# ScalarE instead of GpSimd makes the high weights of twelve units of the delta net's projection

## The reference, cut to what matters

```python
u = rms_norm(h, norm_mix_pre[l])
proj = u @ w_in[l]
dq, dk, dv, dz, db, da, aq, ak, av = jnp.split(proj, split_points, axis=-1)
o_dn = gated_deltanet_group(dq, dk, dv, dz, db, da, conv_w[l], a_log[l], dt_bias[l], dn_out_norm[l])
o_at = axial_gqa_group(aq, ak, av, q_norm[l], k_norm[l])
```

## Time and profile before

| | |
|---|---|
| median of 3 runs | 1503.74 us (1500.91 to 1503.95) |
| the profiled execution | 1504.27 us |
| its span | 1502.2 us |
| TensorE busy | 1393.9 us (93%) |
| VectorE busy | 744.8 us (50%) |
| ScalarE busy | 430.5 us (29%) |
| GpSimd busy | 767.2 us (51%) |
| mean granted clock of TensorE | 0.968 |
| `w_hi` by GpSimd | 188 units, 1071 ns each |
| `w_hi` by ScalarE | 16 units |
| `w_lo` by GpSimd | 204 units, 2530 ns each |

### The profile page before, as it was taken

How to read it: one execution, slowest core, us unless ns; L and a number is a source line. 1 busy time by engine, 2 the same in 40 slices (tenths; PEclk the granted TensorE clock), 3 DMA queues, 4 the chain that set the end, 5 groups by cost and what they waited for, 6 DMA issues and landing times.

```text
span 1502.2 us, 20334 instructions
## 1 busy us (share of the span) xinstructions
PE 1393.9 (93%) x7550; PEld 1144.9 (76%) x7550; DVE 744.8 (50%) x1113; ACT 430.5 (29%) x842; POOL 767.2 (51%) x443
## 2 busy tenths in 40 slices
PE   6999799898999999999899999868989999999996
PEld 4877577677888887888798888648867888888884
DVE  7968566644554457111767886497525111211112
ACT  3253344323121212111344444443423111111111
POOL 5444443345666666666343532405264666666661
PEclk9999899999999999999999999987999999999998
DMA  4321221112322222232111111000031322222221
GB/s 175 101 95 60 67 71 57 57 62 76 117 98 97 93 93 96 96 98 98 46 68 43 57 45 56 29 1 2 9 104 52 102 98 98 98 99 96 92 77 56
DMA packets 31739, 113.86 MB, mean 76 GB/s; under 512 B 3520, under 2 KB 3904, under 8 KB 31424
## 3 DMA queue, kind: packets, MB, share of 16 engines
q1 hardware_dynamic: 31536, 112.85, 22.6%
q10 hardware_dynamic: 144, 0.18, 0.0%
HBM read 110.92 MB, written 2.10 MB: 75 GB/s over the span
## 4 chain that ended last, share of the span: by engine, by line
PE 85%; DVE 10%; ACT 3%; issue 2%; DMA 0%; DVEq 0%; ACTq 0%
PE ps L1025 42%; PE ps L1225 18%; PE ps L1365 6%; PE ps L1044 3%; ACT arena L549 3%; PE ps L1058 2%; PE ps L1245 1%; PE ps L1339 1%; PE ps L1065 1%; PE ps L1168 1%; DVE arena L1665 1%; DVE arena L2038 1%; PE ps L1319 1%; PE ps L1157 1%; DVE arena L2136 1%
## 5 line engine op out<-in xcount | busy, mean ns | idle before, releaser
L470 POOL TENSOR_TENSOR w_lo<-raw,w_hi 128x1024 fp32r<-128x1024 f32 x204 | 516.0, 2530 | 66.1 <-ACT w_hi L549 50.4
L465 POOL TENSOR_SCALAR w_hi<-raw 128x1024 fp32r<-128x1024 f32 x188 | 201.4, 1071 | 565.3 <-PE ps L1025 190.1
L1025 PE MATMUL ps<-h_hi,w_hi 128*128 128x512 f32 (+1 forms) x976 | 376.7, 391 | 4.2 <-DVE arena L2284 2.2
L1025 PE MATMUL ps<-h_lo,w_hi 128*128 128x512 f32 (+1 forms) x976 | 369.8, 384 | 0.0
L1025 PE MATMUL ps<-h_hi,w_lo 128*128 128x512 f32 (+1 forms) x976 | 369.6, 384 | 0.0
L1025 PEld LDWEIGHTS ps<-h_hi,w_hi 128*128 128x128 f32 x976 | 182.4, 189 | 50.0 <-issue 12.1
L1025 PEld LDWEIGHTS ps<-h_lo,w_hi 128*128 128x128 f32 x976 | 182.1, 189 | 37.9 <-issue 2.7
L1025 PEld LDWEIGHTS ps<-h_hi,w_lo 128*128 128x128 f32 x976 | 182.1, 189 | 36.1
L549 ACT ACTIVATE arena<-ps 128x512 f32<-128x512 f32 (+7 forms) x205 | 96.5, 505 | 279.1 <-PE ps L1025 41.9
L549 ACT ACTIVATE arena<-arena 128x512 f32<-128x512 f32 (+6 forms) x191 | 101.4, 534 | 217.7 <-DVE arena L2284 134.3
L1225 PE MATMUL ps<-g_hi,w_hi 128*128 128x512 f32 x400 | 155.7, 389 | 0.9 <-DVE arena L1897 0.9
(11 more groups left out here) (279 smaller groups left out, 1888.5 us busy)
## 6 DMA issues: line engine op xcount, KB each, us to landing
raw<-in_w_stream SPq DMA_DIRECT2D x204, 512.0 KB, 3.5
xT<-in_x_t SPq DMA_DIRECT2D x2, 1056.0 KB, 7.3
out<-xT SPq DMA_DIRECT2D x8, 256.0 KB, 2.1
C<-in_cst SPq DMA_DIRECT2D x1, 576.0 KB, 10.0
arena<-in_cst SPq DMA_DIRECT2D x1, 528.0 KB, 4.9
arena<-in_pos SPq DMA_DIRECT2D x1, 256.0 KB, 3.9
V<-in_vec ACTq DMA_DIRECT2D x1, 174.5 KB, 6.0
band<-in_cst SPq DMA_DIRECT2D x1, 160.5 KB, 3.7
```

Of the source, the lines that this page charges most:

```text
L465: pool.tensor_scalar(w_hi[j][:], raw[j % 2][:], 1.0, 1.0, ALU.mult, ALU.mult).then_inc(S["pool_step"], 1)
L470: pool.tensor_tensor(w_lo[j][:], raw[j % 2][:], w_hi[j][:], ALU.subtract).then_inc(split_done[j], 1)
L1025: last = mm(dst[p], w[:, k, :], h[:, k, cols], start=(k == 0 and n == 0), stop=(k == KT - 1 and n == 2))
```

## The change

`LATE_HIGH` is (30, 33): in rounds 30, 31 and 32, units 120 to 131, GpSimd no longer makes the high part; it waits for `w_high` and makes the low part alone. ScalarE makes the high part of unit `U_DN2 + d + 4` at the end of `dn_copy(d)`, for d = 0 to 11 (for d from 12 on `dn_copy` returns before). Rounds 30 to 33 of GpSimd are written out instead of running in a loop, and later waits for `pool_step` count the three rounds that are left out.

```diff
+        LATE_HIGH = (U_DN2 // 4 + 1, U_DN2 // 4 + 4)
...
-            def split(i):
+            def split(i, late=False):
...
                     if isinstance(i, int) and 1 <= i < HIGH_ROUNDS:
                         pool.wait_ge(S["w_high"], 4 * i + j - 3)
+                    elif isinstance(i, int) and LATE_HIGH[0] <= i < LATE_HIGH[1]:
+                        pool.wait_ge(S["w_high"], 4 * (HIGH_ROUNDS - 1) + 4 * (i - LATE_HIGH[0]) + j + 1)
                     else:
...
-                            pool.wait_ge(S["pool_step"], 4 * i + (j + 1 - 4 * (HIGH_ROUNDS - 1)))
+                            skipped = HIGH_ROUNDS - 1 + (LATE_HIGH[1] - LATE_HIGH[0] if late else 0)
+                            pool.wait_ge(S["pool_step"], 4 * i + (j + 1 - 4 * skipped))
...
-            rep(pool, n0, split, HIGH_ROUNDS)
+            rep(pool, n0 - 1, split, HIGH_ROUNDS)
+            split(n0 - 1)
...
-            with pool.Fori(n0, n, 1) as i:
+            for i in range(n0, n - 1):
                 split(i)
+            split(n - 1, late=True)
...
             with pool.Fori(n, N_UNITS // 4, 1) as i:
-                split(i)
+                split(i, late=True)
...
                 a(y5, x5[:, d % 2, 2:L + 2], ACT.Copy, scale=vcol("dconv", 24 + d)).then_inc(S["c_act"], 1)
+                weight_high(U_DN2 + d + 4)
```

## The result

The changed kernel takes 1505.74 us in the median of 12 runs (1503.58 to 1510.00), the kernel before 1502.99 (12 runs). The ratio is 1.0023, with a 95% interval from 1.0012 to 1.0034: 2 to 5 us slower. I had forecast 0.4 us faster.

What follows compares the result with a forecast made beforehand. TensorE, busy 93% of the span, was taken as the bound. +1.34 (start) - 1.8 (steps 3 and 4) + 0.1 (step 11) + 0 (plain steps) = -0.4 us gave 1503.4 us against the median 1503.74; range 1499.8 to 1506.6.

Steps and rivals of the forecast that it cites:

- The plain step: Ordinary step of the projection loop with the second attention: stays at 10.03 us, costing 0, at most 0.1 us.
- Rival B: ScalarE's copy of the turned probabilities comes late and delays TensorE's turn each step: about +6 us, 1510; chance 0.11.
- C: Rival: VectorE is freed of the high part in every step, up to 1491 us, 1499 given; chance 0.09.
- Rival A: GpSimd wins the tie with VectorE; steps 3 and 4 gain only 0.2 us: +1.5, 1505.3; chance 0.22.
- the tie of step 3: VectorE's convolution step against GpSimd's low part near 825 us; if GpSimd wins, only 0.2 us is gained.
- Step 11: Loop step where VectorE also squares a tile and slack is gone: lateness of 0.07 to 0.4, +0.1 us taken.
- The start, pause: Loop start, TensorE waiting for VectorE's scaling: low part moves back, TensorE restarts 1.34 us later (bounds 0.96 to 1.35).
- The start, clock: TensorE's lower clock after the start's pause: expected the same as before; up to 0.5 us might come back.
- Steps 3 and 4: Convolution steps meeting GpSimd's gate products: 1.2 us shorter pause plus part of 1.25 us of clock; -1.8 taken (0.2 to 2.2).
- The sum: Whole kernel: +1.34 start, -1.8 steps 3 and 4, +0.1 step 11, 0 plain steps: -0.4 us, 1503.4; chance 0.58.
- if the clock falls in other places than before: One of the listed signs that the forecast is wrong, about TensorE's clock; no size given.
- The range: Whole kernel: 1499.8 to 1506.6 us, from bounds -1.7 and +2.5, run spread (2.8 below the median) and part of B.

Runs made afterwards that it cites:

- e5: Kernel before plus one ScalarE copy of 128x1024 into unused space ahead of the first exponentials, GpSimd's work unchanged; 1503.2 us, ratio 0.9998.
- e13: Kernel before plus one ScalarE copy of 128x512 in step 9, delaying TensorE about 0.5 us; 1504.8 us, ratio 1.0016.
- e15: Kernel before plus two ScalarE copies of 128x1024, in steps 8 and 9, delaying TensorE about 2.0 us; 1506.5 us, ratio 1.0024.
- e4: The change, but ScalarE makes unit 120's high part behind the first two heads' exponentials; 1502.7 us, ratio 0.9991 to the kernel before.
- e6: Kernel before plus three ScalarE copies (one 128x1024, two 128x528) ahead of the first exponentials; 1507.5 us, ratio 1.0027.
- e11: The kernel of e6 run once more, unaltered, for another profile; 1507.7 us.
- e1: Kernel before with only unit 120's high part moved to ScalarE, units 121 to 131 left with GpSimd; 1508.8 us, ratio 1.0033.

## Why the prediction was wrong, point by point

- **The plain step** was right: 10.03 us, VectorE won the tie (its step began 0.28 us before GpSimd's and took its plain 0.77), the four steps were 0.03 late (0.07 said), and ScalarE's copy took 1.04. Rival B is out, since the copy that turns the probabilities was not late, and C too. Rival A as it was put (the tie of step 3) did not occur, but a tie of the same kind was lost in step 4.
- **Step 11** cost 0.04 instead of 0.1.
- **The start, pause:** right in size (1.32 us measured, 1.34 said) and in cause: the low part, moved back, holds the scaling until 0.30 us after its own end (790.95 + 2.34 = 793.29, the scaling ends at 793.59), and e5 shows that ScalarE's delay alone costs nothing.
- **The start, clock:** wrong. The prediction said "after a longer pause I expect the same" of the lower clock. The longer pause cost another 1.0 us of it: 6.8 us of the lower clock instead of 3.4. The sum had only a bound for clock time that comes back.
- **Steps 3 and 4:** mis-sized. 1.8 us were taken, 1.4 came. The pause in step 3 shrank by 1.29, as worked out (1.2). The other 0.6 had been put down to the clock that would no longer fall. It did not fall, and TensorE was ready 1.33 us sooner in step 4; but the low part of unit 124 held VectorE's last convolution step (3.11 us instead of 0.77), and all of that went into a pause of 1.53. I had named this meeting and yet let half of the gain through it. VectorE had a lead of 0.19 us there, as in the row where it was held.
- **The sum**, from these terms: +1.3 + 1.0 - 1.4 = +0.9 for the stage instead of -0.4. This is the first failure, and it turns the sign.
- **The rest, 1.5 us of the 2.5 in the mean,** comes from a step that the prediction put at nothing without a word: it let everything behind the stage follow one to one. A fall of the clock behind the pause of 2.21 us costs 1.6 us there in every profile of the change, and e13 to e15 show that a mere delay of 0.6 to 2.0 us brings it. The prediction's own sign, "if the clock falls in other places than before", came in.
- **The range** does not follow from its parts: 1503.74 less 1.7 and less 2.8 is 1499.2, not 1499.8. The measured time is far from that end.

The measured median lies inside the range, which took in +2.5 us; the direction and the chance for slower (0.11) don't hold up, and that the median is inside is luck as far as the mechanism goes. Rival B was slower by a mechanism that didn't occur; the terms that decided were clock time, at the start and behind the stage, and the sum had such time only as something that comes back.

## What to carry to other kernels

Work put on an idle engine costs by its place in that engine's order: here eleven of twelve moved copies cost nothing that could be measured and the one ahead of the first exponentials did, and it cost less by itself than by pushing back another engine's operation that excludes VectorE's. When TensorE already pauses for microseconds, price a longer pause as the pause and the clock behind it; and when a later part of the kernel has pauses, also of 2 us, a small shift ahead of it is not paid one to one. Look for that in several profiles of each kernel, divided at the same pauses: what is the same in all (here 1.6 us) is a cost, what differs between profiles of one kernel (here up to 3.6 us) is not to be read from one of them. Before moving work off an engine to relieve a wait, look for the instructions that are in the way in exactly that wait: the gate products here, not the high parts.

## What the runs showed of the hardware that was not expected

- The lower clock at the loop's start began 0.3 us after TensorE's restart in the kernel before (pause of 4.06 us), 1.3 us after it in e4 (3.05), and 1.1 us before it in the change (5.38), by the trace's clock records. With a pause of 3.0 to 4.1 us it lasted 3.4 us, with 5.4 us 6.8 us, and with 5.06 us once the one and once the other (e6, e11).
- A pause of 2.3 us in step 3 was followed by a lower clock in the kernel before and by none in e1 and e11. A pause of 2.21 us behind the loop was followed by none in five profiles and by 3.4 us of it in thirteen, always the same for the same kernel.
- With 0.28 us of lead VectorE kept its instruction in every plain step, and GpSimd's took 2.72 instead of 2.40 us. This agrees with the rule of the Trainium skill quoted in the prediction ("SBUF — State Buffer", section "Who interferes with whom"). The lead alone does not tell who wins: with 0.19 us VectorE was held twice (837.49 in the earlier trace rows, 842.79 in the change), and with 0.16 us it was not. VectorE in e4, ahead of the low part of 790.53 shown above, which took 2.84:

```profile
790.37 0.77 DVE L2048 SCALAR_TENSOR_TENSOR arena<-arena,V 128x528 f32<-128x528 f32 x1
```

Where VectorE was held, GpSimd had come straight from its instruction before; where it was not, GpSimd had been idle. Whether that is what decides, no run tests.
